# Attention scores of two heads issued in turn on the upper and lower 64 rows of TensorE

## What is computed

```python
h = rms_norm(x, norm1_g); z = h @ w_in            # pool (512) | q (8x64) | k (2x64) | v (2x64)
q = apply_axial_rope(rms_norm(q, q_norm_g)) * ATTN_SCALE
k = apply_axial_rope(rms_norm(k, k_norm_g))
s = jnp.einsum('bqkgd,bskd->bkgqs', qblk, k)      # 128-query blocks, 4 query heads to a key head
p = jax.nn.softmax(s, axis=-1)
o = jnp.einsum('bkgqs,bskd->bqkgd', p, v)
x = x + jnp.concatenate([pool_mixer(zp), o], -1) @ w_out
x = x + peer_ffn(rms_norm(x, norm2_g), ...)       # product-key retrieval over 128*128 experts
```

## Time and profile before

| | us |
|---|---|
| median of three runs | 1971.09 |
| lowest, highest | 1969.82, 1972.81 |
| span of the profiled execution | 1973.0 |
| TensorE busy in it | 1951.1 (99%) |
| VectorE, ScalarE, GpSimd busy | 1642.5, 977.3, 838.5 |
| attention, first score product to output projection | 118.33 to 212.56 |

### The profile page before, as it was taken

The page is one execution under the profiler, slowest core; times in us unless marked ns, Lnnn a source line. Parts: engine busy times, 40 slices in busy tenths (PEclk is TensorE's granted clock), DMA queues, the critical chain, the costliest instruction groups (busy, mean ns, idle before and its releaser), DMA issues.

```text
span 1973.0 us, 28846 instructions
## 1 busy us (share of the span) xinstructions
PE 1951.1 (99%) x10204; PEld 1660.6 (84%) x10204; DVE 1642.5 (83%) x3148; ACT 977.3 (50%) x2043; POOL 838.5 (42%) x588
## 2 busy tenths in 40 slices
PE   8999999999999999999999999999999999999999
PEld 8977998987888888888888888788888888788887
DVE  3866436879999999999977776898988999889898
ACT  4266243324787787787877772332222222223231
POOL 0334102001333333433455655555666566666563
PEclk9999999999999999999999999999999999999999
DMA  6110312225789989989899999999999999999996
GB/s 267 43 36 1 139 54 107 79 88 196 232 301 326 300 311 311 321 296 303 299 378 397 401 411 406 362 343 406 390 405 388 407 401 406 399 407 404 406 399 256
DMA packets 203366, 581.27 MB, mean 295 GB/s; under 512 B 19936, under 2 KB 57184, under 8 KB 201056
## 3 DMA queue, kind: packets, MB, share of 16 engines
q0 software_dynamic: 73728, 268.47, 36.6%
q1 hardware_dynamic: 60192, 180.12, 24.5%
q10 hardware_dynamic: 69312, 130.97, 17.6%
HBM read 505.03 MB, written 74.45 MB: 294 GB/s over the span
## 4 chain that ended last, share of the span: by engine, by line
PE 63%; DMA 17%; DVE 11%; issue 4%; POOL 2%; ACT 2%; SPq 0%; ACTq 0%; DVEq 0%
PE ps L334 19%; PE ps L335 18%; PE ps L336 18%; DMA ring_a<-in_v,expert_ids 7%; PE ps L1516 5%; DMA ring_b<-in_v,expert_ids 5%; DVE sparse L1191 2%; DMA ring_c<-in_v,expert_ids 2%; DMA gel_dram<-arena_b 1%; PE ps L1390 1%; DVE arena_a L1215 1%; DVE v_lo_slots_b L1203 1%; POOL ring_c L833 1%; PE ps L1477 1%; DVE v_lo_slots_a L1203 1%
## 5 line engine op out<-in xcount | busy, mean ns | idle before, releaser
L334 PE MATMUL ps<-v_hi_slots,w_lo 128*128 128x512 f32 x1024 | 399.2, 390 | 2.5 <-DVE w_lo L1221 2.3
L336 PE MATMUL ps<-v_hi_slots,w_lo 128*128 128x512 f32 x1024 | 398.4, 389 | 0.0
L334 PE MATMUL ps<-feat_hi,w_hi 128*128 128x512 f32 (+1 forms) x936 | 360.1, 385 | 1.5 <-DVE w_lo L1093 1.1
L335 PE MATMUL ps<-feat_lo,w_hi 128*128 128x512 f32 (+1 forms) x936 | 351.2, 375 | 0.0
L336 PE MATMUL ps<-feat_hi,w_lo 128*128 128x512 f32 (+1 forms) x936 | 351.0, 375 | 0.0
L722 ACT ACTIVATE w_lo<-arena_a 128x512 fp32r<-128x512 f32 x128 | 81.0, 633 | 493.6 <-DVE arena_a L1215 371.4
L833 POOL DMA_INDIRECT ring_a<-in_u_rows,expert_ids x86 | 123.2, 1432 | 320.4 <-DVE ring_a L1183 186.1
L334 PEld LDWEIGHTS ps<-v_hi_slots,w_lo 128*128 128x128 f32 x1024 | 192.2, 188 | 45.0 <-DVE w_lo L1221 5.3
L336 PEld LDWEIGHTS ps<-v_hi_slots,w_lo 128*128 128x128 f32 x1024 | 192.2, 188 | 40.2
L336 PEld LDWEIGHTS ps<-feat_hi,w_lo 128*128 128x128 f32 x936 | 176.2, 188 | 31.8
L334 PEld LDWEIGHTS ps<-feat_hi,w_hi 128*128 128x128 f32 x936 | 176.6, 189 | 30.9 <-DVE w_lo L1093 1.9
(11 more groups left out here) (223 smaller groups left out, 4469.5 us busy)
## 6 DMA issues: line engine op xcount, KB each, us to landing
arena_a<-in_v ACTq DMA_DIRECT2D x121, 512.0 KB, 7.7
w_raw<-in_uT SPq DMA_DIRECT2D x85, 512.0 KB, 6.5
g_dram<-arena_a ACTq DMA_DIRECT2D x64, 512.0 KB, 8.4
gel_dram<-arena_b ACTq DMA_DIRECT2D x120, 256.0 KB, 5.4
w_raw<-gel_dram SPq DMA_DIRECT2D x120, 256.0 KB, 8.2
arena_a<-in_uT SPq DMA_DIRECT2D x43, 512.0 KB, 6.8
w_raw<-in_w_all SPq DMA_DIRECT2D x16, 1024.0 KB, 5.8
arena_b<-g_dram SPq DMA_DIRECT2D x32, 512.0 KB, 11.8
```

The source lines that it names most:

```text
L334: nc.tensor.matmul(out, lh, rh, start=first, stop=False)
L335: nc.tensor.matmul(out, lh, rl, start=False, stop=False)
L336: return nc.tensor.matmul(out, ll, rh, start=False, stop=last)
```

## The change

The two heads of a feature tile and query tile become neighbours. `units` now lists (head 0, head 1) of one query tile after another, so `scores(j, p)` makes a pair of units: six matmuls, in which head 0 (rows 0 to 63, bank `p % 2 * 2`) and head 1 (rows 64 to 127, the next bank) take turns. Scores use four banks instead of three, turned probabilities two (`4 + u % 2`) instead of three. `PTh` gets a place of its own in `arena_a`, `PTh` and `PTl` have four slots. A group is now four units, and `values(j, g)` makes both heads' products in one go, 24 matmuls (12 for the narrow group). There are three groups to a feature tile instead of six; the batch of 256 tokens is finished in the second group, so its output comes first (`1 - q` in the waits). ScalarE's loop over the feature tiles is written out.

```diff
-        groups = [(0, 0, 0), (1, 0, 0), (0, 0, 1), (0, 2, 0), (0, 2, 1), (1, 0, 1)]
-        units = [(q, hh, t + i) for q, t, hh in groups for i in range(2)]
+        groups = [(0, 0), (1, 0), (0, 2)]
+        units = [(q, hh, t + i) for q, t in groups for i in range(2) for hh in range(2)]
...
+        def turned(j, u):
+            return (j * NG + u // 4) % 2 * 2 + u % 2, slice(u % 4 // 2 * P, (u % 4 // 2 + 1) * P)
...
             def pt_out(j, u):
-                if u % 2 == 0:
-                    act.wait_ge(pv_mm, j * NG + (u // 2 + 1))
+                slot, cols = turned(j, u)
+                if u % 4 == 0 and j * NG + u // 4 >= 2:
+                    act.wait_ge(pv_mm, j * NG + u // 4 - 1)
                 act.wait_ge(p_tr, j * NU + (u + 5))
...
-                    if u in (2, 5) and not first:
-                        o_out(j - 1, u // 5)
+                    if u in (2, 5) and not first:
+                        o_out(j - 1, 1 - u // 5)
...
-            def scores(j, u):
-                q, hh, t = units[u]
-                pe.wait_ge(exp_ok, j * NU + (u + 1))
-                pe_split_product(ps[:, u % 3, 0:n * P], FTh[rows, j, cols], FTl[rows, j, cols], kTh[rows, keys],
-                                 kTl[rows, keys], True, True).then_inc(qk_mm, 1)
+            def scores(j, p):
+                q, _, t = units[2 * p]
+                if j * NU + 2 * p >= 4:
+                    pe.wait_ge(exp_ok, j * NU + 2 * p - 2)
+                for i, (qT, kT) in enumerate(((FTh, kTh), (FTh, kTl), (FTl, kTh))):
+                    for hh in range(2):
+                        rows = slice(64 * hh, 64 * hh + 64)
+                        ins = mm(ps[:, p % 2 * 2 + hh, 0:n * P], qT[rows, j, cols], kT[rows, keys],
+                                 start=i == 0, stop=i == 2)
+                        if i == 2:
+                            ins.then_inc(qk_mm, 1)
...
             def values(j, g):
-                pe.wait_ge(pt_lo, j * NU + (2 * g + 5))
+                pe.wait_ge(pt_lo, 2 + j * NU + 4 * g + 4)
+                for hh in range(2):
+                    slot, feats = (j * NG + g) % 2 * 2 + hh, slice(64 * hh, 64 * hh + P)
+                    for s in range(n):
+                        last = pe_split_product(ps[:, 6 + q, t * P:(t + 2) * P], Vh[:, t0 + s, feats],
+                                                Vl[:, t0 + s, feats], PTh[slot][:, s, :], PTl[slot][:, s, :],
+                                                hh == s == 0, hh == 1 and s == n - 1)
...
+                for p in range(NU // 2):
+                    if p:
+                        flip(j, 2 * p - 1)
+                    elif not first:
+                        flip(j - 1, NU - 1)
+                    if p + 2 < NU // 2:
+                        scores(j, p + 2)
+                    elif j < 3:
+                        scores(j + 1, p + 2 - NU // 2)
+                    flip(j, 2 * p)
+                    if p == 1 and not first:
+                        values(j - 1, 2)
+                    if p % 2 == 1 and p >= 3:
+                        values(j, p // 2 - 1)
```

More of the change, by code:

```diff
@@ L164, in build @@
         qkr = view(A_, 13824, TT, QK)
-        PTh, PTl = (view(w, 0, 2, 4, 2 * P) for w in (Wh_, Wl_))
+        PTh = [view(PTh_, 1024 * i, 4, 2 * P) for i in range(4)]
+        PTl = [view(w, 1024 * i, 4, 2 * P) for w in (Wh_, Wl_) for i in range(2)]
         qpT = view(A_, 6144, 2, 2, TOK)
@@ L603, in pair @@
                     if u in (2, 5) and not first:
-                        o_out(j - 1, u // 5)
+                        o_out(j - 1, 1 - u // 5)
             pair(0, True)
-            with act.Fori(1, 4) as j:
+            for j in range(1, 4):
                 pair(j)
@@ L610, in _ @@
                 pt_out(3, u)
+            o_out(3, 1)
             o_out(3, 0)
-            o_out(3, 1)
             for n in range(6, 10):
@@ L1394, in values @@
             def values(j, g):
-                q, hh, t = units[2 * g]
+                q, t = groups[g]
                 t0, n = SEQ_TILES[q]
-                pe.wait_ge(pt_lo, j * NU + (2 * g + 5))
[L1398 to L1403, removed]
+                pe.wait_ge(pt_lo, 2 + j * NU + 4 * g + 4)
+                pe.wait_ge(o_lo, j * 2 + 2 - q)
+                for hh in range(2):
[4 more added lines that the diff above has]
+                                                hh == s == 0, hh == 1 and s == n - 1)
                 last.then_inc(pv_mm, 1)
@@ L1407, in pair @@
                 if first:
[L1408 to L1411, removed]
+                    scores(j, 0)
+                    pe.wait_ge(mix_lo, 6)
+                    scores(j, 1)
                     windows(3)
-                for u in range(NU):
-                    if u + 3 < NU:
-                        scores(j, u + 3)
+                for p in range(NU // 2):
[5 more added lines that the diff above has]
+                        scores(j, p + 2)
                     elif j < 3:
-                        scores(j + 1, u + 3 - NU)
-                    if first and u == 0:
+                        scores(j + 1, p + 2 - NU // 2)
+                    if first and p == 0:
                         group_map(3)
-                    if first and u == 5:
+                    flip(j, 2 * p)
+                    if first and p == 3:
                         pe.wait_ge(mix_lo, 8)
                         pe.wait_ge(v_parts, 2)
-                    if u >= 1:
-                        flip(j, u - 1)
-                    elif not first:
-                        flip(j - 1, NU - 1)
-                    if u in (1, 3) and not first:
-                        values(j - 1, NG - 2 + u // 2)
-                    if u >= 5 and u % 2 == 1:
-                        values(j, u // 2 - 2)
+                    if p == 1 and not first:
+                        values(j - 1, 2)
+                    if p % 2 == 1 and p >= 3:
+                        values(j, p // 2 - 1)
             pair(0, True)
@@ L1435, in _ @@
             flip(3, NU - 1)
[L1436 to L1437 removed]
+            values(3, 2)
             pe.wait_ge(o_lo, 2 + 6)
```

46 lines of the change are left out of this document (21 added, 25 removed).

## The result

The changed kernel takes 1964.63 us, the median of 5 runs (1962.93 to 1967.08), beside 1971.09 us for the kernel before on the same chip. The ratio is 0.996 with a 95% interval of 0.9949 to 0.9972: 6.5 us less, with bounds of 5.5 and 10. In a second set of runs it took 1964.79 beside 1971.86, ratio 0.9961 (0.9949 to 0.9974). The forecast was 1960.8, a gain of 10.3. Sign and range held. The gain is about two thirds of what I had worked out.

A forecast was written before the change was run, and what follows sets the result against it. TensorE, busy all 22.61 us of a tile, was taken to bound the attention part. Start, three tiles of 18.8 us and end put its finish at 202.2 instead of 212.56: 1971.1 - 10.3 = 1960.8 us, range 1957.5 to 1970.5.

The forecast's parts named there:

- Bound: Attention part: TensorE, busy 22.61 of 22.61 us a tile, sets it; its gain passes to the end in full.
- Part 1: Score and values blocks of a tile: fewer blocks cut entering and leaving costs from 4.3 to 2.4, saving 1.9 us.
- Part 2: Score pairs: two heads stream together, each needing its own load every 0.11; 1.12 us wide, 1.02 narrow; chance 0.50.
- both rivals that denied it: Score pairs: heads stream one behind the other (1968.6 us, chance 0.17), or each change of half drains (1987.6, chance 0.10).
- no overlap: Score pairs: heads stream one behind the other, 1.72 us wide and 1.07 narrow; 1968.6 us in all; chance 0.17.
- drains: Score pairs: every change of half empties the array, 0.40 a matmul, wide pair 2.57 us; 1987.6 in all; chance 0.10.
- rival of hidden loads: Score pairs: loads hide too, 1.03 us wide or 0.71 narrow, mostly lost to waits; 1959.0 in all; chance 0.15.
- Part 3: Two banks for turned probabilities: two flips loop in 2.06 us against TensorE's 1.86, so it waits 0.2 once a tile.
- Part 4: Behind the first batch's values: a 2.36 us chain from the output copy against 1.75 of TensorE work, 0.6 wait.
- Part 5: Attention's start and end: start 13.3 of work plus 1.5 of waits, end 9.8; attention ends at 202.2, not 212.56.
- Sum: Whole kernel: a 10.3 us gain gives 1962.7 us for the profiled execution and 1960.8 for the median.

The follow-up runs named there:

- same_rows: The changed kernel with both heads' score matmuls on rows 0 to 63, the first head's computed twice: 1969.73 us, ratio 0.9989 to the kernel before.
- heads_not_in_turn: The changed kernel with head 0's three score matmuls of a pair issued first, then head 1's three: 1963.08 us, ratio 0.9948 to the kernel before.

## Why the prediction was right, and where its sizes were off

**Bound.** TensorE set the attention part, and the gain passed to the end: the projection starts at 202.89 and what stands behind it took 1758.2 us, no more than the 1760.5 of before.

**Part 1, fewer blocks.** Forecast 1.9 us a tile. By same_rows it is 22.61 - 21.13 = 1.5 with its hidden waits, 2.0 by the tile without them (20.6). It holds.

**Part 2, side by side.** The mechanism held against both rivals that denied it: no overlap measures 1.57 and 0.91, the changed kernel 0.90 and 0.55, and nothing drains between the halves. The size was too high. I charged a load each 0.11 for 0.95 and 0.85; four loads stand in 0.30, so the narrow pair, whose streams are short, was off by 0.30. With the wide one's 0.05 that is 0.8 a tile too much work. The Trainium skill (TensorE: Matmul & The Clock Gate, Part 3) has row groups run at once, and by it I had 0.86 for a wide block up to its transposes and 0.54 for a narrow one: the trace agrees, 0.90 and 0.55. The rival of hidden loads was the true one for this term. The same section says that matmuls start and end in program order; heads_not_in_turn speaks against it where the row groups differ. The prediction took one thing more from there, that a load passes a running matmul only where its row group differs. The rows of before do not bear it out: a load on the same rows starts at 127.21, between the matmuls of 127.11 and 127.45.

**Part 3, two banks.** This is the step that failed by most: 0.2 us a tile forecast, 1.2 measured (0.30 + 0.60 + 0.32). Three things were missized. VectorE's remainder ends at 142.08 + 0.69 = 142.77 and TensorE starts at 142.91, so the handoff back is 0.14, not 0.05. The loop is 2.1 to 2.45 us, not 2.06: 142.91 - 140.81 = 2.1; 138.91 - 136.68 = 2.2; 144.34 - 141.89 = 2.45, where VectorE takes an output's remainder and a maximum between two remainders of probabilities (142.08 and 143.51). And TensorE's iteration got shorter than I put it (a narrow one 142.31 - 140.81 = 1.50, not 1.86), so each of three iterations waits, not one. I had said this in the rival of hidden loads ("most of it goes into the waits") without giving it more than 0.15.

**Part 4, the queue behind the output.** Forecast 0.6, measured 1.02, the cause as named. From 147.69, where TensorE leaves the values, to 150.34 the chain takes 2.65 instead of 2.36. Its steps lasted as priced (output 147.89 to 148.38, exponential to 148.83, copy 0.60, remainder 0.67); the handoffs were too small: 0.20 to ScalarE, 0.10 to VectorE and 0.14 back, 0.44 instead of 0.13. TensorE's own work in between, 149.32 - 147.69 = 1.63, was 0.12 shorter than put.

**Part 5, both ends.** End 9.8 behind the last full values, measured 202.89 - 193.1 = 9.8, with 0.59, 0.80 and 1.41 of waits. Start 14.8 forecast, 14.65 at a full clock, 15.7 as it ran. The rows of before show no such fall, and no wait of TensorE in that stretch.

**Sum.** Of the 2.2 us by which the attention part missed its forecast, 1.3 are the tiles (1.0 less work, 1.4 more waits, three times) and 0.9 the start. That work and wait were off by 1.0 and 1.4 and nearly cancelled is luck, not precision. The median missed the forecast by 3.8 us. The 1.6 that are left over lie in the rest of the program, where single executions differ by as much, and I have no cause for them. The profiled execution says the reverse, 1961.1 where 1962.7 was forecast, because the stretches ahead of the part and behind it were shorter than in the profile before.

## What to carry to other kernels

Matmuls of 64 rows on the two halves of the array run side by side if they stand together in the queue, here up to three places apart: six with 512 columns in 0.90 us instead of 1.57. When such a step makes an engine's stages shorter but not the loop through the other engines, put the shorter time into each iteration of that loop and see which of them still cover it; then spread the work that hides it, here values in halves, for another 8 us (7.5 of the attention part at equal clock). Read waits from the distance of starts, since the drawn length of a short matmul hides waits of up to 0.2 us, and check the releaser that a trace names against what the waiting instruction asks for in the program, and not only against the time at which it ended.

## What the runs showed of the hardware that I had not expected

- A matmul on the other half of the rows started beside one of the first half, with more of the first half's still ahead of it in the program (heads_not_in_turn: four `feat_hi` before any `feat_lo`, four loads in 0.30 us, the first matmuls of the two heads within 0.01 us of each other).
- VectorE's end reached TensorE 0.14 us later; the forecast had 0.02 to 0.05 for each handoff.
- TensorE's clock fell to its lower level for a few microseconds behind waits of 0.51, 0.69 and 0.44 us in three of three executions of the changed kernel, and in none of five of three other kernels with the same work in that stretch. It cost about 1.05 us.
